# Sparse attention of a float32 two-network kernel: packed fp32r scores, the causal mask as a TensorE product, and one exit for each head

## The chip, the cores and the metric

The kernel runs on one core of one Trainium2 chip, as one launch. The metric is device time in microseconds. The program computes two small transformer networks, one after the other, with two layers each, in float32 on 512 tokens of width 1024.

## What is computed

The part that the change touches is ordinary softmax attention with a causal mask, in three places. The reference of network two's sparse attention, cut to what matters (its compressed branch, the choice of blocks and the window are left out):

```python
q = rope(q.reshape(b, t, N_NSA, D), positions).reshape(b, t, G, R, D)      # 6 heads in 2 groups, D = 64
s_s = einsum('bqgrd,bgqnd->bgrqn', qb, k_sel).astype(f32) * scale          # scores, selected keys
p_s = masked_softmax(s_s, key_pos <= tq[:, None])
o_s = einsum('bgrqn,bgqnd->bqgrd', p_s, v_sel)
s_w = einsum('bqgrd,bngd->bgrqn', qb, kw).astype(f32) * scale              # scores, window keys
p_w = masked_softmax(s_w, m_w)
o_w = einsum('bgrqn,bngd->bqgrd', p_w, vw)
return gt[:, :, 0] * o_c + gt[:, :, 1] * o_s + gt[:, :, 2] * o_w
```

With 512 tokens the kernel treats the selected branch and the window branch both as full causal attention. Network one has a latent attention of 8 heads (causal) and an attention of 4 heads over the best keys of each query (causal, and masked by an index search).

## The kernel before

All tokens lie on 128 partitions in TT = 4 tiles. Big projections run elsewhere, as three fp32r products each (`product`, L262: high by high, high by low, low by high). The attention stages use plain float32.

`softmax_attention` (L2277) is used three times, with the names mla (8 heads, 32 units), dsa (4 heads, 16 units) and nsa (12 heads: 6 for the selected keys and 6 for the window keys; 48 units). A unit is one head and one tile t of 128 queries, with (t + 1) x 128 keys. Each engine has its own instruction list and they meet by semaphores only:

- TensorE, in iteration i: the scores of unit i (L2305) into one of four PSUM banks; the transposes of the probabilities of unit i − 2 (L2314), after ScalarE's exponential of that unit; the product with the values of unit i − 4 (L2325), after ScalarE's copy of the transposed probabilities (L2377), and after the exit of unit i − 6 (`kept`). At the end of a stage come 8 filler transposes (`stay_busy`, L162).
- VectorE, in iteration i: it adds the mask to the last 128 columns of the scores in PSUM (L2340; in dsa to all columns, for tiles above 0), takes the negative maximum (L2341), and then does the exit of unit i − 5: reciprocal of the row sum (L2348), and scaling of the 128x64 result (L2351), or, with a gate, scaling by two factors (L2353) and the addition to what is there (L2354).
- ScalarE, in iteration i: the exponential with its row sum (L2368), then the copy of the transposed probabilities of unit i − 2 (L2377).

After `step(...)` an engine waits for its own instruction.

In network two the stage `turned_and_compressed` (L3087, named cmp) comes before nsa. It turns 15 tiles from token-major to transposed form on TensorE (`turns`: 0 to 3 compressed keys and values, 4 to 6 queries, 7 and 8 selected keys, 9 and 10 window keys, 11 to 14 the queries and keys of the next attention). Even ones are kept by ScalarE (L3221), odd ones by VectorE (L3252). Keys of a group stand twice, once in each half of the partitions, with zeros in the other half that GpSimd clears (L3130), so that a score product runs over 128 rows with two heads' queries in the stationary operand. Then come the compressed attention's scores (L3190, after VectorE's small copy L3263), 26 filler transposes, ScalarE's exponential (L3240), VectorE's mask (L3281), and for each of 6 heads the transposes (L3203), ScalarE's copy (L3243), the product with the values (L3212) and VectorE's exit (L3290, one 128x256 multiplication by a broadcast factor).

## Time and profile before

| | |
|---|---|
| timed runs, median (lowest to highest) of 3 | 3373.87 us (3372.31 to 3375.93) |
| the profiled execution: span | 3368.7 us |
| VectorE busy | 1884.3 us (56% of the span) |
| ScalarE busy | 1311.1 us (39%) |
| nsa, first layer: first score product to last exit | 1666.47 to 1746.16 us |
| nsa, second layer: first score product | 2613.17 us |

The span is that of one execution taken by the hardware profiler; the timed runs are others. The compression stage of the first layer begins at 1624.3 us and that of the second at 2574.1 us. Busy shares of TensorE count a product's whole passage, so a share near 100% does not say that the array works at its peak; the distance from one start to the next says what a product costs in a row of them.

### The profile page before, as it was taken

How to read it: one execution, taken by the hardware profiler on the slowest of the kernel's cores; microseconds unless marked ns; L12 is line 12 of the kernel's file. 1: busy time of each engine (PE TensorE's matmuls, PEld its weight loads, DVE VectorE, ACT ScalarE, POOL GpSimd, SP SyncE). 2: the span in 40 equal slices, each digit the busy share in tenths (PEclk: the TensorE clock that was granted, in tenths of full speed). 3: DMA queues.
4: the chain of work that ended last, by engine and by line, in shares of the span. 5: the costliest groups of instructions: out<-in, count | busy, mean ns of one | idle time of the engine just before them, and what ended most of it. 6: DMA issues, size and time to landing. Idle time of an engine off the chain costs nothing. (4 is left out here: it accounts for less than half of the span.)

```text
span 3368.7 us, 49442 instructions
## 1 busy us (share of the span) xinstructions
PE 3198.9 (95%) x19200; PEld 2657.4 (79%) x19200; DVE 1884.3 (56%) x3610; ACT 1311.1 (39%) x2780; POOL 394.5 (12%) x368
## 2 busy tenths in 40 slices
PE   8998999999989999979999999999899989999996
PEld 6877888877777888868867888888788768888885
DVE  4875443336865434247486457474475865574644
ACT  4455433334354424134363333233443543332324
POOL 1021000000030000003013302010012034010100
PEclk9999999999999999989899999999999999999998
DMA  4111222222102222132100122222222000222221
GB/s 166 54 51 38 88 100 88 88 77 86 66 1 76 100 97 91 38 123 94 51 1 2 40 71 100 97 99 85 81 97 74 1 1 5 91 94 102 91 99 42
DMA packets 37345, 239.58 MB, mean 71 GB/s; under 512 B 4464, under 2 KB 5232, under 8 KB 15088
## 3 DMA queue, kind: packets, MB, share of 16 engines
q1 hardware_dynamic: 36528, 234.21, 19.5%
q8 instruction: 158, 2.59, 0.3%
q10 hardware_dynamic: 576, 2.10, 0.2%
q14 instruction: 83, 0.68, 0.1%
HBM read 234.19 MB, written 2.10 MB: 70 GB/s over the span
## 5 line engine op out<-in xcount | busy, mean ns | idle before, releaser
L265 PE MATMUL ps<-b_hl,bff_whl 128*128 128x512 f32 x704 | 274.1, 389 | 3.1 <-DVE b_hl L630 3.1
L267 PE MATMUL ps<-b_hl,bff_whl 128*128 128x512 f32 x704 | 273.9, 389 | 0.0
L266 PE MATMUL ps<-b_hl,bff_whl 128*128 128x512 f32 x704 | 273.9, 389 | 0.0
L248 DVE SCALAR_TENSOR_TENSOR bff_whl<-ring,b_cols,bff_whl 128x512 fp32r<-128x512 f32 (+1 forms) x224 | 153.2, 745 | 197.3 <-ACT bff_whl L235 197.0
L245 DVE TENSOR_TENSOR aff_whl<-ring,aff_whl 128x512 fp32r<-128x512 f32 x160 | 99.8, 686 | 223.1 <-ACT aff_whl L233 223.1
L235 ACT ACTIVATE bff_whl<-ring,b_cols 128x512 fp32r<-128x512 f32 (+1 forms) x224 | 136.6, 682 | 176.4 <-PE ps L267 176.4
L266 PE MATMUL ps<-aff_whl,a_u 128*128 128x512 f32 x512 | 204.3, 399 | 0.0
L265 PE MATMUL ps<-a_hl,aff_whl 128*128 128x512 f32 x512 | 199.4, 390 | 3.1 <-DVE a_hl L630 3.1
L265 PE MATMUL ps<-aff_whl,a_u 128*128 128x512 f32 x512 | 201.7, 394 | 0.0
L267 PE MATMUL ps<-aff_whl,a_u 128*128 128x512 f32 x512 | 200.7, 392 | 0.0
L266 PE MATMUL ps<-a_hl,aff_whl 128*128 128x512 f32 x512 | 199.2, 389 | 0.0
L267 PE MATMUL ps<-a_hl,aff_whl 128*128 128x512 f32 x512 | 199.2, 389 | 0.0
L265 PE MATMUL ps<-ain_whl,a_hl 128*128 128x512 f32 (+3 forms) x512 | 189.3, 370 | 9.4 <-issue 6.2
L233 ACT CAST aff_whl<-ring 128x512 fp32r<-128x512 f32 x160 | 87.5, 621 | 275.9 <-PE ps L267 271.3
L266 PE MATMUL ps<-ain_whl,a_hl 128*128 128x512 f32 (+3 forms) x512 | 186.2, 364 | 0.0
L267 PE MATMUL ps<-ain_whl,a_hl 128*128 128x512 f32 (+3 forms) x512 | 186.0, 363 | 0.0
L245 DVE TENSOR_TENSOR bff_whl<-ring,bff_whl 128x512 fp32r<-128x512 f32 x128 | 84.6, 720 | 144.2 <-ACT bff_whl L233 144.2
L265 PEld LDWEIGHTS ps<-b_hl,bff_whl 128*128 128x128 f32 x704 | 132.1, 188 | 30.9 <-DVE b_hl L630 3.6
L248 DVE SCALAR_TENSOR_TENSOR aff_whl<-ring,a_gains,aff_whl 128x512 fp32r<-128x512 f32 x128 | 87.6, 746 | 122.3 <-ACT aff_whl L235 122.1
L267 PEld LDWEIGHTS ps<-b_hl,bff_whl 128*128 128x128 f32 x704 | 132.2, 188 | 27.6
L266 PEld LDWEIGHTS ps<-b_hl,bff_whl 128*128 128x128 f32 x704 | 132.2, 188 | 27.3
L233 ACT CAST bff_whl<-ring 128x512 fp32r<-128x512 f32 x128 | 70.4, 621 | 210.3 <-PE ps L267 202.8
(510 smaller groups left out, 7826.8 us busy)
## 6 DMA issues: line engine op xcount, KB each, us to landing
ring<-in_a_w_ff SPq DMA_DIRECT2D x64, 1024.0 KB, 4.6
ring<-in_b_w_up SPq DMA_DIRECT2D x32, 1024.0 KB, 4.8
ring<-in_a_w_in SPq DMA_DIRECT2D x16, 1024.0 KB, 4.9
ring<-in_b_w_down SPq DMA_DIRECT2D x16, 1024.0 KB, 4.6
ring<-in_b_w_in_att SPq DMA_DIRECT2D x12, 1024.0 KB, 4.6
ring<-in_b_w_up SPq DMA_DIRECT2D x16, 768.0 KB, 4.1
ring<-in_b_w_in_conv SPq DMA_DIRECT2D x12, 768.0 KB, 4.2
ring<-in_a_w_out SPq DMA_DIRECT2D x8, 1024.0 KB, 4.7
```

What stands on the lines that cost most here:

```text
L233: self.c.nc.scalar.copy(self.part(j, 0, k), src[:, k, :]).then_inc(self.hi_made, 1)
L235: self.c.nc.scalar.activation(self.part(j, 0, k), src[:, k, :], ACT.Copy, scale=g[:, row + k:row + k + 1]).then_inc(self.hi_made, 1)
L245: self.c.nc.vector.tensor_tensor(self.part(j, 1, k), src[:, k, :], self.part(j, 0, k).bitcast(F32), ALU.subtract).then_inc(self.lo_made, 1)
L248: self.c.nc.vector.scalar_tensor_tensor(out=self.part(j, 1, k), in0=src[:, k, :], scalar=g[:, row + k:row + k + 1], in1=self.part(j, 0, k) ...
L265: nc.tensor.matmul(bank, sh, mh, start=start, stop=False)
L266: nc.tensor.matmul(bank, sh, ml, start=False, stop=False)
L267: return nc.tensor.matmul(bank, sl, mh, start=False, stop=stop)
```

## The change

- `softmax_attention` takes heads instead of units. The results of a head's four tiles go side by side into one PSUM bank (128x256), and VectorE makes one exit for a head, after the maximum of the first tile two heads later: reciprocal of four sums, with a gate a product with it, one multiplication by the broadcast factor and, with a gate, one addition. This holds for mla, dsa and nsa.
- In nsa the queries are split into a high and a low fp32r part, and both stand one above the other in the 128 rows of the stationary operand. The keys' high part stands in both halves, their low part in the half of the queries' high part, with zeros in the other. Two single fp32r products then make a score; the product of the two low parts is not in it.
- In nsa a third fp32r product, the identity by the 128x128 mask, adds the mask in PSUM; VectorE adds none.
- The compression stage makes these operands: ScalarE the high parts, VectorE the low parts, and VectorE copies the identity and the mask to fp32r.

```diff
-def softmax_attention(c, name, units, meanwhile=None, first_act=None):
+class AttentionHead:
+    def __init__(self, scores, values, masks, out, gate=None):
+        self.scores, self.values, self.masks, self.out, self.gate = scores, values, masks, out, gate
+def softmax_attention(c, name, heads, meanwhile=None, first_act=None, mask_product=None):
     nc = c.nc
+    units = [(h, t) for h in range(len(heads)) for t in range(TT)]
     U = len(units)
     with ExitStack() as ctx:
         sb = lambda n, s: ctx.enter_context(nc.sbuf_tensor(name + n, s, F32))
         p, pT = sb("p", [P, 3, SEQ]), sb("pT", [P, 2, SEQ])
-        negmax, rsum, rinv = sb("negmax", [P, 8]), sb("rsum", [P, 8]), sb("rinv", [P, 8])
-        tmp = sb("o", [P, 2, HD])
+        negmax, rsum, weight = sb("negmax", [P, 8]), sb("rsum", [P, 4, TT]), sb("weight", [P, 2, TT])
+        tmp = sb("o", [P, 2, TT, HD])
         with c.stage(name, "scores", "maxed", "probs", "turned", "probsT", "outs", "kept", "step", "pool_step",
                      "act_first") as (
                 block, scores, maxed, probs, turned, probsT, outs, kept, step_sem, pool_step, act_first):
@@ -2299,32 +2311,37 @@
             def _(pe):
                 for i in range(U + 4):
                     if i < U:
-                        qT, kT = units[i][0], units[i][1]
+                        h, t = units[i]
+                        nk = (t + 1) * P
                         if i >= 4:
                             pe.wait_ge(probs, i - 3)
-                        nc.tensor.matmul(c.ps[:, i % 4, 0:kT.shape[1]], qT, kT,
-                                         start=True, stop=True).then_inc(scores, 1)
+                        pairs = heads[h].scores(t)
+                        for n, (q, k) in enumerate(pairs):
+                            ins = nc.tensor.matmul(c.ps[:, i % 4, 0:nk], q, k, start=(n == 0),
+                                                   stop=(n == len(pairs) - 1 and mask_product is None))
+                        if mask_product is not None:
+                            ins = nc.tensor.matmul(c.ps[:, i % 4, nk - P:nk], mask_product[0], mask_product[1],
+                                                   start=False, stop=True)
+                        ins.then_inc(scores, 1)
                     u = i - 2
                     if 0 <= u < U:
-                        nk = units[u][1].shape[1]
                         pe.wait_ge(probs, u + 1)
                         if u >= 2:
                             pe.wait_ge(probsT, u - 1)
-                        for j in range(nk // P):
+                        for j in range(units[u][1] + 1):
                             ins = nc.tensor.transpose(c.ps[:, 4 + u % 2, j * P:(j + 1) * P],
                                                       p[:, u % 3, j * P:(j + 1) * P], c.ident)
                         ins.then_inc(turned, 1)
                     u = i - 4
                     if 0 <= u < U:
-                        nb = units[u][1].shape[1] // P
+                        h, t = units[u]
                         pe.wait_ge(probsT, u + 1)
-                        if u >= 2:
-                            pe.wait_ge(kept, u - 1)
-                        for j in range(nb):
-                            v = units[u][2](j)
-                            ins = nc.tensor.matmul(c.ps[:, 6 + u % 2, 0:v.shape[1]],
-                                                   pT[:, u % 2, j * P:(j + 1) * P], v,
-                                                   start=(j == 0), stop=(j == nb - 1))
+                        if t == 0 and h >= 2:
+                            pe.wait_ge(kept, h - 1)
+                        for j in range(t + 1):
+                            ins = nc.tensor.matmul(c.ps[:, 6 + h % 2, t * HD:(t + 1) * HD],
+                                                   pT[:, u % 2, j * P:(j + 1) * P], heads[h].values(j),
+                                                   start=(j == 0), stop=(j == t))
                         ins.then_inc(outs, 1)
                 c.stay_busy(pe, 0, 8)
@@ -2333,27 +2350,28 @@
                 step = Steps(dve, step_sem)
                 for i in range(U + 5):
                     if i < U:
-                        mask, nk = units[i][3], units[i][1].shape[1]
+                        h, t = units[i]
+                        nk, mask = (t + 1) * P, heads[h].masks(t)
                         dve.wait_ge(scores, i + 1)
-                        nm = mask.shape[1]
-                        s = c.ps[:, i % 4, nk - nm:nk]
-                        step(nc.vector.tensor_tensor(s, s, mask, ALU.add))
+                        if mask is not None:
+                            s = c.ps[:, i % 4, nk - mask.shape[1]:nk]
+                            step(nc.vector.tensor_tensor(s, s, mask, ALU.add))
                         nc.vector.tensor_reduce(negmax[:, i % 8:i % 8 + 1], c.ps[:, i % 4, 0:nk],
                                                 AX.X, ALU.max, negate=True).then_inc(maxed, 1)
                     u = i - 5
-                    if 0 <= u < U:
-                        out, gate, add = units[u][4:7]
-                        ri = rinv[:, u % 8:u % 8 + 1]
+                    if 0 <= u < U and units[u][1] == TT - 1:
+                        h = units[u][0]
+                        head, w = heads[h], weight[:, h % 2, :]
+                        wide = w.unsqueeze(2).broadcast_to([P, TT, HD])
+                        o = c.ps[:, 6 + h % 2, 0:TT * HD].rearrange("p (t d) -> p t d", t=TT)
                         dve.wait_ge(outs, u + 1)
-                        step(nc.vector.reciprocal(ri, rsum[:, u % 8:u % 8 + 1]))
-                        o = c.ps[:, 6 + u % 2, 0:out.shape[1]]
-                        if gate is None:
-                            nc.vector.tensor_scalar(out, o, ri, None, ALU.mult).then_inc(kept, 1)
-                        elif add:
-                            step(nc.vector.tensor_scalar(tmp[:, u % 2, :], o, ri, gate, ALU.mult, ALU.mult))
-                            nc.vector.tensor_tensor(out, out, tmp[:, u % 2, :], ALU.add).then_inc(kept, 1)
+                        step(nc.vector.reciprocal(w, rsum[:, h % 4, :]))
+                        if head.gate is None:
+                            nc.vector.tensor_tensor(head.out, o, wide, ALU.mult).then_inc(kept, 1)
                         else:
-                            nc.vector.tensor_scalar(out, o, ri, gate, ALU.mult, ALU.mult).then_inc(kept, 1)
+                            step(nc.vector.tensor_tensor(w, w, head.gate, ALU.mult))
+                            step(nc.vector.tensor_tensor(tmp[:, h % 2], o, wide, ALU.mult))
+                            nc.vector.tensor_tensor(head.out, head.out, tmp[:, h % 2], ALU.add).then_inc(kept, 1)
             @block.scalar
             def _(act):
@@ -2361,16 +2379,19 @@
                     first_act(act, act_first)
                 for i in range(U + 3):
                     if i < U:
-                        nk = units[i][1].shape[1]
+                        h, t = units[i]
+                        nk = (t + 1) * P
                         act.wait_ge(maxed, i + 1)
                         if i >= 3:
                             act.wait_ge(turned, i - 2)
+                        if t == 0 and h >= 4:
+                            act.wait_ge(kept, h - 3)
                         nc.scalar.activation(p[:, i % 3, 0:nk], c.ps[:, i % 4, 0:nk], ACT.Exp,
                                              bias=negmax[:, i % 8:i % 8 + 1],
-                                             accum_out=rsum[:, i % 8:i % 8 + 1]).then_inc(probs, 1)
+                                             accum_out=rsum[:, h % 4, t:t + 1]).then_inc(probs, 1)
                     u = i - 2
                     if 0 <= u < U:
-                        nk = units[u][1].shape[1]
+                        nk = (units[u][1] + 1) * P
                         act.wait_ge(turned, u + 1)
                         if u >= 2:
                             act.wait_ge(outs, u - 1)
...
+    by_act = [i for i in range(len(turns)) if i % 2 == 0 or i in split]
+    by_dve = [i for i in range(len(turns)) if i % 2 or i in split]
...
-                    for dst, src in halves(i):
-                        ins = nc.scalar.activation(dst, src, ACT.Copy, scale=turns[i][2])
+                    if i in split:
+                        ins = nc.scalar.copy(turns[i][1].hi, c.ps[:, i % 4, :])
+                    else:
+                        for dst, src in halves(i):
+                            ins = nc.scalar.activation(dst, src, ACT.Copy, scale=turns[i][2])
                     ins.then_inc(act_kept, 1)
+                def query_high(f):
+                    r = own_half(f)
+                    nc.scalar.copy(qhl[r, f // 2, f % 2, :], qT[r, f // 2, :]).then_inc(q_his, 1)
...
+                keep(7)
                 keep(8)
                 silu(1)
+                keep(9)
                 keep(10)
                 for i in range(12, len(turns), 2):
                     keep(i)
+                wait_kept(act, 4)
+                wait_kept(act, 5)
+                wait_kept(act, 6)
+                for f in range(2):
+                    query_high(f)
...
+                for f in range(2, H):
+                    query_high(f)
...
+                    if i in split:
+                        dve.wait_ge(act_kept, by_act.index(i) + 1)
+                        keys = turns[i][1]
+                        for b in range(2):
+                            r = own_half(b)
+                            ins = nc.vector.tensor_tensor(keys.lo[r, b, :], c.ps[r, i % 4, :],
+                                                          keys.hi[r, :].bitcast(F32), ALU.subtract)
...
+                def query_low(f):
+                    r, to = own_half(f), other_half(f)
+                    dve.wait_ge(q_his, f + 1)
+                    nc.vector.tensor_tensor(qhl[to, f // 2, f % 2, :], qT[r, f // 2, :],
+                                            qhl[r, f // 2, f % 2, :].bitcast(F32), ALU.subtract).then_inc(q_los, 1)
...
-                for i in (1, 3, 5, 7, 9):
+                for i in (1, 3, 5, 7, 8, 9):
                     keep(i)
                 dve.wait_ge(small, 1)
                 nc.vector.tensor_copy(kcT[:], c.ps[:, SMALL, 128:128 + G * N]).then_inc(small_kept, 1)
+                keep(10)
...
+                for a, b in zip(mask_product, (c.ident, c.causal)):
+                    nc.vector.tensor_copy(a[:], b)
                 for h in range(H):
+                    query_low(h)
                     dve.wait_ge(outs, h + 1)
...
+            qhl = sb1r("qhl", [P, NSA_H // 2, 2, SEQ])
+            khi, klo = sb1r("khi", [P, 2, NSA_G, SEQ]), sb1r("klo", [P, 2, NSA_G, 2, SEQ])
...
+            mask_product = sb1r("identr", [P, P]), sb1r("causalr", [P, P])
...
-                turns += [(twice(a + g * HD), (kT[0:HD, g, 0, :], kT[HD:P, g, 1, :]), 1.0)
-                          for a, kT in ((B_KS, ksT), (B_KW, kwT)) for g in range(NSA_G)]
+                turns += [(twice(a + g * HD), SplitKeys(khi[:, i, g, :], klo[:, i, g]), 1.0)
+                          for i, a in ((0, B_KS), (1, B_KW)) for g in range(NSA_G)]
...
-                pads = [kT[r, :, b, :] for kT in (ksT, kwT) for r, b in ((slice(HD, P), 0), (slice(0, HD), 1))]
-                turned_and_compressed(c, "cmp", turns, pads, cols["w2"], cols["pe"], kv2T, qT, gates, out4)
-            units = []
-            for i, (kT, v) in enumerate(((ksT, B_VS), (kwT, B_VW))):
-                for h in range(NSA_H):
-                    g = h // NSA_R
-                    for t in range(TT):
-                        units.append((qT[:, h // 2, t * P:(t + 1) * P], kT[:, g, h % 2, 0:(t + 1) * P],
-                                      lambda j, v=v, g=g: proj[:, j, v + g * HD:v + (g + 1) * HD], c.causal,
-                                      out4[:, t, h, :], gates[:, t, (i + 1) * NSA_H + h:(i + 1) * NSA_H + h + 1], True))
-            softmax_attention(c, "nsa", units)
+                pads = [klo[r, :, :, b, :].bitcast(F32) for r, b in ((slice(HD, P), 0), (slice(0, HD), 1))]
+                turned_and_compressed(c, "cmp", turns, pads, cols["w2"], cols["pe"], kv2T, qT, qhl, gates, out4,
+                                      mask_product)
+            def packed_scores(i, h):
+                q, g = qhl[:, h // 2, h % 2], h // NSA_R
+                return lambda t: [(q[:, t * P:(t + 1) * P], khi[:, i, g, 0:(t + 1) * P]),
+                                  (q[:, t * P:(t + 1) * P], klo[:, i, g, h % 2, 0:(t + 1) * P])]
+            softmax_attention(c, "nsa", [
+                AttentionHead(packed_scores(i, h),
+                              lambda j, a=v + h // NSA_R * HD: proj[:, j, a:a + HD], lambda t: None,
+                              out4[:, :, h, :], gates[:, :, (i + 1) * NSA_H + h])
+                for i, v in enumerate((B_VS, B_VW)) for h in range(NSA_H)],
+                mask_product=(mask_product[0][:], mask_product[1][:]))
```

## Rows read from the trace of the kernel before

**Rows 1.** Page part 1: busy us of each engine, share of the span, instructions.

```profile
PE 3198.9 (95%) x19200; PEld 2657.4 (79%) x19200; DVE 1884.3 (56%) x3610; ACT 1311.1 (39%) x2780; POOL 394.5 (12%) x368
```

**Rows 2.** Busy by stretch: length, PE, PEld, DVE, ACT, POOL, granted clock, DMA, GB/s.

```profile
1658.00:1667.00 9.00, 8.22 (x36) 6.91 (x36) 1.70 (x4) 1.15 (x2) 0.00 (x0) 0.50 0.00 0
...
1667.00:1677.00 10.00, 9.34 (x41) 6.01 (x39) 6.55 (x21) 5.42 (x19) 0.00 (x0) 0.77 0.01 2
...
1717.00:1727.00 10.00, 9.75 (x60) 7.25 (x60) 8.81 (x34) 6.11 (x20) 0.00 (x0) 1.00 0.00 1
```

**Rows 3.** Timeline, nsa, layer one: start, length, engine, line, instruction, count [idle before].

```profile
1690.44 0.44 PE L2305 MATMUL ps<-b_ksT,b_qT 128*128 128x128 f32 x2
...
1691.24 0.29 DVE L2340 TENSOR_TENSOR ps<-ps,const_b 128x128 f32<-128x128 f32 x1
...
1691.47 0.41 PE L2325 MATMUL ps<-b_proj,nsapT 128*128 128x64 f32 x2 [0.26 <-DVE b_mix L2354]
...
1691.56 0.29 DVE L2341 TENSOR_REDUCE nsanegmax<-ps 128x1 f32<-128x128 f32 x1
...
1691.77 0.15 DVE L2348 RECIPROCAL nsarinv<-nsarsum 128x1 f32<-128x1 f32 x1
...
1692.34 0.23 DVE L2354 TENSOR_TENSOR b_mix<-b_mix,nsao 128x64 f32<-128x64 f32 x1
...
1692.48 0.29 DVE L2340 TENSOR_TENSOR ps<-ps,const_b 128x128 f32<-128x128 f32 x1
...
1696.75 0.44 PE L2305 MATMUL ps<-b_ksT,b_qT 128*128 128x128 f32 x2
```

**Rows 4.** Timeline of mla, first layer.

```profile
221.87 1.08 PE L2305 MATMUL ps<-a_kT,a_qT 96*128 96x512 f32 x2
...
222.78 0.38 PE L2314 MATMUL ps<-const_a,mlap 128*128 128x128 f32 x2
...
223.84 0.44 PE L2305 MATMUL ps<-a_kT,a_qT 96*128 96x128 f32 x2
...
224.12 0.49 PE L2314 MATMUL ps<-const_a,mlap 128*128 128x128 f32 x3
...
227.53 1.08 PE L2305 MATMUL ps<-a_kT,a_qT 96*128 96x512 f32 x2
```

**Rows 5.** Timeline of dsa, second layer.

```profile
1002.70 1.08 PE L2305 MATMUL ps<-a_kbT,a_qbT 128*128 128x512 f32 x2
...
1008.82 1.08 PE L2305 MATMUL ps<-a_kbT,a_qbT 128*128 128x512 f32 x2
```

**Rows 6.** Timeline of the compression stage, second layer: its exit.

```profile
2602.74 0.42 DVE L3290 TENSOR_TENSOR b_mix<-ps,cmpst 128x256 f32<-128x256 f32 x1 [0.80 <-PE ps L3212]
```

**Rows 7.** Timeline of a projection of network two, TensorE alone: products in fp32r.

```profile
1500.11 0.39 PE L267 MATMUL ps<-b_hl,bin_whl 128*128 128x512 f32 x1
...
1500.34 0.39 PE L265 MATMUL ps<-b_hl,bin_whl 128*128 128x512 f32 x1
```

**Rows 8.** Timeline of mla: products with the values.

```profile
223.00 1.00 PE L2325 MATMUL ps<-a_proj,mlapT 128*128 128x64 f32 x8
```

**Rows 9.** Timeline of the compression stage, both layers.

```profile
1656.47 0.62 PE L3203 MATMUL ps<-const_b,cmps 128*31 128x128 f32 x4
...
1658.14 1.06 PE L3203 MATMUL ps<-const_b,cmps 128*31 128x128 f32 x4
...
1661.02 1.06 PE L3203 MATMUL ps<-const_b,cmps 128*31 128x128 f32 x4
...
2589.76 1.39 DVE L3252 TENSOR_SCALAR b_kwT<-ps 64x512 f32<-64x512 f32 x2 [4.34 <-PE ps L3147]
...
2590.63 1.20 ACT L3221 ACTIVATE b_kwT<-ps 64x512 f32<-64x512 f32 x2 [1.40 <-PE ps L3147]
...
2598.40 0.82 ACT L3240 ACTIVATE cmps<-cmps 128x744 f32<-128x744 f32 x1
...
2600.90 1.05 ACT L3243 COPY cmppT<-ps 31x512 f32<-31x512 f32 x2 [1.68 <-PE ps L3203]
```

More of the change, by code:

```diff
@@ L3084, in _, with __init__, turned_and_compressed @@
                     dve.wait_ge(states, t + 1)
-def turned_and_compressed(c, name, turns, pads, w2, pe_tiles, kv2T, qT, gates, out):
+class SplitKeys:
+    def __init__(self, hi, lo):
+        self.hi, self.lo = hi, lo
+def turned_and_compressed(c, name, turns, pads, w2, pe_tiles, kv2T, qT, qhl, gates, out, mask_product):
     nc = c.nc
+    split = [i for i in range(len(turns)) if isinstance(turns[i][1], SplitKeys)]
+    by_act = [i for i in range(len(turns)) if i % 2 == 0 or i in split]
+    by_dve = [i for i in range(len(turns)) if i % 2 or i in split]
     H, G, N = NSA_H, NSA_G, N_CMP
@@ L3108, in turned_and_compressed, with own_half, other_half @@
         with c.stage(name, "turned", "act_kept", "dve_kept", "pe_here", "biased", "silus", "small", "small_kept",
[L3109 removed]
+                     "scores", "step", "centred", "exps", "masked", "p_turned", "p_kept", "outs", "outs_kept", "padded", "q_his", "q_los") as (
                 block, turned, act_kept, dve_kept, pe_here, biased, silus, small, small_kept, scores, step_sem, centred,
[L3111 removed]
+                exps, masked, p_turned, p_kept, outs, outs_kept, padded, q_his, q_los):
             def wait_kept(engine, i):
[L3113 to L3116 removed]
+                if i in by_dve:
+                    engine.wait_ge(dve_kept, by_dve.index(i) + 1)
+                else:
+                    engine.wait_ge(act_kept, by_act.index(i) + 1)
+            def own_half(f):
+                return slice(HD * (f % 2), HD * (f % 2 + 1))
+            def other_half(f):
+                return slice(HD * (1 - f % 2), HD * (2 - f % 2))
             def halves(i):
@@ L3555, in first_block @@
                 softmax_attention(c, "mla", [
-                    (qT[0:MLA_QK, h, t * P:(t + 1) * P], kT[0:MLA_QK, h, 0:(t + 1) * P],
-                     lambda j, h=h: kv4[:, j, h, MLA_NOPE:], c.causal,
-                     mix[:, t, h * MLA_V:(h + 1) * MLA_V], None, False)
-                    for h in range(MLA_H) for t in range(TT)], other_ropes)
+                    AttentionHead(lambda t, h=h: [(qT[0:MLA_QK, h, t * P:(t + 1) * P],
+                                                   kT[0:MLA_QK, h, 0:(t + 1) * P])],
+                                  lambda j, h=h: kv4[:, j, h, MLA_NOPE:], lambda t: c.causal,
+                                  mix[:, :, h * MLA_V:(h + 1) * MLA_V])
+                    for h in range(MLA_H)], other_ropes)
             with ExitStack() as ctx3:
@@ L3584, in first_block @@
                           lambda dve, step, i: search.late(dve, step, i, TOPK // 8 - SEARCH_EARLY))
-                units = []
-                for h in range(DSA_H):
-                    for t in range(TT):
-                        mask = c.causal if t == 0 else search.tile(t)
-                        units.append((qbT[:, h // 2, t * P:(t + 1) * P],
-                                      kbT[:, h % 2, 0:(t + 1) * P],
-                                      lambda j: proj[:, j, A_AV:A_AV + DSA_D], mask,
-                                      mix[:, t, o_b + h * DSA_D:o_b + (h + 1) * DSA_D], None, False))
+                sparse = [AttentionHead(lambda t, h=h: [(qbT[:, h // 2, t * P:(t + 1) * P],
+                                                         kbT[:, h % 2, 0:(t + 1) * P])],
+                                        lambda j: proj[:, j, A_AV:A_AV + DSA_D],
+                                        lambda t: search.tile(t) if t else c.causal,
+                                        mix[:, :, o_b + h * DSA_D:o_b + (h + 1) * DSA_D]) for h in range(DSA_H)]
                 junk = sb3("junk", [P, HD])
@@ L3601, in last_spread @@
                                              accum_out=var[:, t, h:h + 1]).then_inc(spreads, 1)
-                softmax_attention(c, "dsa", units,
+                softmax_attention(c, "dsa", sparse,
                                   lambda pool, step: group_norm(nc, pool, step, out4, heads(A_RG, RET_H, RET_D),
@@ L3713, in attentions @@
                           for a, dst, s in ((B_SQ, sqT, HD ** -0.5), (B_SK, skT, 1.0)) for i in range(SB_H // 2)]
-                pads = [kT[r, :, b, :] for kT in (ksT, kwT) for r, b in ((slice(HD, P), 0), (slice(0, HD), 1))]
-                turned_and_compressed(c, "cmp", turns, pads, cols["w2"], cols["pe"], kv2T, qT, gates, out4)
-            units = []
-            for i, (kT, v) in enumerate(((ksT, B_VS), (kwT, B_VW))):
-                for h in range(NSA_H):
-                    g = h // NSA_R
-                    for t in range(TT):
-                        units.append((qT[:, h // 2, t * P:(t + 1) * P], kT[:, g, h % 2, 0:(t + 1) * P],
-                                      lambda j, v=v, g=g: proj[:, j, v + g * HD:v + (g + 1) * HD], c.causal,
-                                      out4[:, t, h, :], gates[:, t, (i + 1) * NSA_H + h:(i + 1) * NSA_H + h + 1], True))
```

13 lines of the change are left out of this document (5 added, 8 removed).

## The prediction, made before the kernel was changed

> **What bounds the kernel now.** I read the page's busy line first: the reader is to see TensorE at 95% of the span and VectorE at 56% [rows 1]. The chain of waits was no help, since it stays within the last microsecond of the program. An average over two networks does not say what one attention stage is worth, so I read busy time by stretches. In network two's sparse attention (the stage named nsa, twice in the span, 48 units of work each time) TensorE is 9.75 of 10 us busy and VectorE 8.81 of 10; the stretch just before it stands at a granted clock of 0.50, that is 1.2 GHz [rows 2].
>
> Two engines near full need the timeline. One head (four units, one for each tile of 128 queries) takes 1696.75 − 1690.44 = 6.31 us of nsa. In it the probabilities-by-values product waits for VectorE's last write [0.26 <-DVE b_mix] [rows 3]. VectorE's starts there give what one exit (reciprocal, scaling, addition) costs: reciprocal to addition 0.57, addition to the next mask addition 0.14, sum 0.71 us; and mask addition to maximum 0.32 us. The same loop in network one's first attention (mla), with a shorter exit and nothing waiting, runs a head in 227.53 − 221.87 = 5.66 us [rows 4]. There one step follows another on TensorE: the score product of 128 keys takes 0.28 us and that of 512 keys 0.91 us; between them on a line, 0.49 and 0.70 for 256 and 384, together 2.38 us. The rest, 5.66 − 2.38 = 3.28 us, is transposes and products with the values. So mla is TensorE's own pace, and nsa is 0.65 us a head over that pace because of VectorE. The top-k attention (dsa) takes 1008.82 − 1002.70 = 6.12 us a head, 0.46 over it, with the same VectorE in front: its mask additions are wide [rows 5].
>
> **The change, part by part.**
>
> *Mask and exits leave VectorE.* In nsa, four mask additions go (4 × 0.32 = 1.28 us a head) and four exits become one. The new exit is a reciprocal (0.15 as in [rows 3], 0.19 with the wait for its own end), a product with the gate on four numbers a row (about the same, 0.19), a 128x256 multiplication out of PSUM by a broadcast factor, which the compression stage already does in 0.42 us [rows 6], and an addition of the same size, 0.42 at most: 1.22 us with no waits, against 4 × 0.71 = 2.84. VectorE had 6.31 × 0.881 = 5.6 us a head; it now has 5.6 − 1.28 − 1.62 = 2.7 us. It cannot be the bound any more.
>
> *Scores.* Each full float32 product goes as two TensorE instructions. The new score is two single-pass fp32r products over all 128 rows, and a third of 128 columns for the mask. The big products of the kernel run in fp32r at 1500.34 − 1500.11 = 0.23 us for 512 columns, 0.44 ns a column [rows 7]. The six wide products of a head (2 × (256 + 384 + 512) = 2304 columns) cost 1.02 us. The six narrow ones (two scores of 128 keys, four masks) have no row in fp32r. Bounds: 0.057 us each by columns alone; 0.28 us if a narrow fp32r product is worth a whole float32 one [rows 4]. The nearest row is the value product: eight loads of 128x128 weights with 64 columns each take 1.00 us [rows 8]; two of them take 0.41 [rows 3], so a pair of load and product is (1.00 − 0.41)/6 = 0.10 us, set by the load. I take 0.107: 0.64 us for six. Scores are then 1.66 us, with 0.1 for seams 1.76. A head of TensorE: 3.28 + 1.76 = 5.04 us.
>
> The Trainium skill (TensorE: Matmul & The Clock Gate, section on the back-to-back issue gap) has pairs of load and product of 128 columns at about 81 ns. By that the six cost 0.49 us, and the whole change would bring some 3 us more; my row is of float32 weights and doesn't settle it.
>
> *Does anything else take TensorE's place?* ScalarE is the candidate: four exponentials with their sums and four copies. I laid one head out in TensorE's order (scores of unit i, transposes of i − 2, values of i − 4). The delicate point is the exit, now 1.22 us in one piece between the maxima of tiles 0 and 1. The second maximum ends 2.4 us after the head's start, the exponential 0.5 later, and the transposes that need it come at 4.0. The copy of tile 3 ends at 3.5 and is needed at 4.2. Slack is 0.6 us or more everywhere, so I take 5.04 us. Gain 6.31 − 5.04 = 1.27 a head. Eleven heads run in the steady state (the first fills the pipe at the low clock): 14.0 us, and 1.0 for shorter scores in the filling. The last exit, uncovered at the end of the stage, is 1.22 against 0.71: −0.5. Per layer 14.5 us, for two layers **29.0 us gained**.
>
> *mla and dsa* get only shared exits. In mla TensorE was never kept waiting: nothing. Its last exit is longer by 0.14 us and lies beside the filler transposes. In dsa VectorE falls below TensorE's 5.66, so 0.46 × 3 heads after filling × 2 layers = **2.8 us gained**.
>
> *The compression stage pays for the operands.* Keys are kept by both ScalarE (high part, one copy of 128x512 instead of two of 64x512) and VectorE (low part, two subtractions of 64x512). ScalarE's two copies took 1.20 us, so one is 0.6; VectorE's pair 1.39 [rows 9]. The last key tile's low part now starts after its high part: the small copy of compressed keys behind it, which TensorE's compressed scores await, is late by 0.6 us. Then two query copies stand in ScalarE's queue ahead of the exponential: 1.2 us. Four more (2.4 us) stand between the exponential and the first probability copy. These started 2600.90 − 2598.40 = 2.50 after one another; now the exponential's 0.82 plus 2.4 make 3.22: 0.7 more. Sum 2.5 us. VectorE's query remainders (0.69 each, one a head) and the two copies of the mask's operands (0.3 each, as the 128x128 mask addition) fit in its waits for TensorE of 0.8 to 2.5 us: nothing, and if that cover were gone 0.7 us a head. GpSimd clears the same bytes with half the instructions.
>
> The price has a second part. TensorE waits some 2 us longer in that stage with its fillers used up, and the granted clock there already falls to half [rows 2]. One head's step there took 1.67 us just before (1656.47 to 1658.14) and 2.88 after (to 1661.02) [rows 9]; each step that falls under the low clock earlier costs 1.2 us. I take one a layer, bounds 0 and 3. The skill's page just named, in the section on the clock gate, says that throttled is the default and activity releases it; taken alone, that speaks against this change, since it makes TensorE idle. It would give the upper bound, 3.7 us a layer; the trace shows also that the clock had fallen in a stretch with TensorE 8.22 of 9 us busy, so idling alone is not all of it. Together 2.5 + 1.1 = 3.6 us a layer, **7.2 us lost** (5 to 12.5).
>
> **Sum.** −29.0 − 2.8 + 7.2 = −24.6 us on the profiled 3368.7: 3344.1 us of span. The median of the timed runs, 3373.87, is 5.2 over that span; I carry it over: 3349 us.
>
> **Rivals.**
> - *Narrow fp32r runs at four cycles a column* (0.23 us, what 512 columns cost now). For it: float32 takes that much per column. Against: nothing in the trace has fp32r under 256 columns. Heads at 5.04 + 6 × 0.12 = 5.76; 15.8 us less gain over 22 heads: 3365 us.
> - *The exit in one piece stalls the pipe.* If my slack is wrong by more than 0.6 us, the loop is paced by maximum, exit, maximum, exponential, copy, and loses about 0.5 us a head: 3360 us. For it: TensorE waited for VectorE before. Against: the layout above.
> - *It does not do what it says*: the narrow products cost a whole float32 product, 0.28 us. Scores are 1.02 + 1.68 + 0.1 = 2.80, more than the 2.38 removed; a head takes 6.08, gain 0.23, and the compression stage eats it: 3372 us, no change.
> - *Slower:* nsa's TensorE stays at 1.2 GHz. The stage starts at half clock and the mean rose to 0.77 in its first 10 us [rows 2], under dense float32 passes. Lighter fp32r work in its place with gaps might not raise it. TensorE's 5.04 then becomes about 10 us: 5 lost on each head that stays low. It decides from about five heads of 24 (24.6/5) on; all of a layer would be 3400 us. Against: the fp32r layers run at full clock throughout.
>
> **How the numbers follow.** Forecast 0.66, its own range 3341 to 3356. Four cycles a column 0.13; stalling exit 0.10; whole float32 price 0.07; low clock 0.04. Between 3340 and 3366 lies all of the first three but their edges. A change of 0.2% (6.7 us) is about what a measurement can tell here: faster 0.87, same 0.08, slower 0.05.
>
> **What would show it.** In the profile after: no mask addition of nsa on VectorE and 24 exits of 128x256; a head of nsa at 5.0 us, with no wait of the value products on VectorE; 128-column fp32r starts 0.11 apart; mla's head still 5.66, dsa's near 5.7; the compression stage 2.5 to 6 us longer, with ScalarE's query copies ahead of its exponential. A head above 5.5 us, or a nsa stretch with granted clock under 1.0 beyond its first 10 us, makes the prediction wrong.

## The result, and the profile after

The changed kernel takes 3342.74 us (median of 4 runs, 3337.18 to 3348.88), the kernel before on the same chip 3374.43 (4 runs, 3372.31 to 3375.93): ratio 0.9915 [0.9897, 0.9933], 31.7 us less. Timed twice more, each time beside the kernel before, it took 3357.00 (12 runs, 3346.07 to 3364.95; before 3365.66, ratio 0.9963 [0.9947, 0.9979]) and 3353.58 (6 runs, 3344.83 to 3359.12; before 3369.39, ratio 0.9949 [0.9929, 0.9969]). So the gain is 9, 16 or 32 us, and the forecast of 25 lies between. The scatter is not measuring noise alone: TensorE's granted clock falls for some microseconds at places that the change does not touch, in some executions and not in others.

The page of the kernel after, part 1 (compare [rows 1]):

```profile
span 3335.4 us, 49102 instructions
...
PE 3166.2 (95%) x19296; PEld 2662.0 (80%) x19296; DVE 1816.9 (54%) x3202; ACT 1313.6 (39%) x2792; POOL 393.7 (12%) x364
```

VectorE lost 408 instructions and 67 us of work; TensorE stays at 95%. Stretches of nsa, first layer, columns as in [rows 2]:

```profile
1662.00:1671.00 9.00, 8.22 (x36) 7.03 (x36) 3.76 (x7) 1.15 (x2) 0.00 (x0) 0.50 0.00 0
1671.00:1681.00 10.00, 10.00 (x68) 9.72 (x68) 4.67 (x12) 6.97 (x25) 0.00 (x0) 0.77 0.01 2
...
1701.00:1711.00 10.00, 10.00 (x89) 9.84 (x88) 6.18 (x18) 7.20 (x24) 0.00 (x0) 1.00 0.01 2
```

TensorE is busy 10.00 of 10 us, where it was 9.75; VectorE 6.18, where it was 8.81. The entry at half clock and the rise in the first 10 us are as before. One head of nsa in the timeline (columns as in [rows 3]):

```profile
1694.28 0.31 PE L2320 MATMUL ps<-b_khi,b_qhl 128*128 128x128 f32 x1
...
1694.42 0.27 PE L2320 MATMUL ps<-b_klo,b_qhl 128*128 128x128 f32 x1
...
1694.54 0.28 PE L2323 MATMUL ps<-b_causalr,b_identr 128*128 128x128 f32 x1
...
1694.65 0.52 PE L2332 MATMUL ps<-const_b,nsap 128*128 128x128 f32 x3
...
1695.46 0.42 DVE L2373 TENSOR_TENSOR nsao<-ps,nsaweight 128x256 f32<-128x256 f32 x1
...
1695.92 0.42 DVE L2374 TENSOR_TENSOR b_mix<-b_mix,nsao 128x256 f32<-128x256 f32 x1
...
1697.54 0.47 PE L2320 MATMUL ps<-b_khi,b_qhl 128*128 128x512 f32 x1
...
1697.85 0.39 PE L2320 MATMUL ps<-b_klo,b_qhl 128*128 128x512 f32 x1
1697.85 0.19 PEld L2323 LDWEIGHTS ps<-b_causalr,b_identr 128*128 128x128 f32 x1
1698.07 0.22 PE L2323 MATMUL ps<-b_causalr,b_identr 128*128 128x128 f32 x1
...
1698.13 0.39 PE L2332 MATMUL ps<-const_b,nsap 128*128 128x128 f32 x2
...
1699.17 0.31 PE L2320 MATMUL ps<-b_khi,b_qhl 128*128 128x128 f32 x1
```

A head is 1699.17 − 1694.28 = 4.89 us, no mask addition is left on VectorE, and no TensorE row waits. Where the time went, by stages, in us for each layer. The marks are starts of instructions: compression runs from its first one to nsa's first maximum, nsa from there to the first row of the stick-breaking attention behind it ("stick") that writes its scores to SBUF, and stick from there to its last addition in PSUM; "rest" is all else:

| kernel | compression | nsa | stick | rest | span |
|---|---|---|---|---|---|
| before | 43.3 + 40.2 | 79.6 + 79.2 | 45.9 + 45.0 | 3035.5 | 3368.7 |
| after | 46.9 + 46.0 | 63.5 + 63.4 | 40.3 + 41.9 | 3033.4 | 3335.4 |

nsa gave 31.9 us and the compression stage took 9.4: together 22.5. A further 8.7 came from stick, whose code is the same; no part of the forecast had it.

### The profile page after: what moved, and what is told of

Read it like the earlier page. It is cut to its first block and busy times, and to the rows that moved or that the text cites. A ratio compares the mean times of both kernels' runs of the same rounds, so it can differ in the third digit from the quotient of the medians.

```text
span 3335.4 us, 49102 instructions
## 1 busy us (share of the span) xinstructions
PE 3166.2 (95%) x19296; PEld 2662.0 (80%) x19296; DVE 1816.9 (54%) x3202; ACT 1313.6 (39%) x2792; POOL 393.7 (12%) x364
```

## The experiments

### Which of the three edits does it (six kernels)

**Shared exits alone**, on the kernel before; scores and mask additions stay:

```diff
-                    if 0 <= u < U:
+                    if 0 <= u < U and units[u][1] == TT - 1:
...
-                        step(nc.vector.reciprocal(ri, rsum[:, u % 8:u % 8 + 1]))
+                        step(nc.vector.reciprocal(w, rsum[:, h % 4, :]))
```

> The kernel before with the shared exits alone, in all three attention stages; scores in plain float32, mask on VectorE. Theory (nsa was held by VectorE's waits, and TensorE's own pace with float32 scores is 5.66 us a head): VectorE falls from 5.6 to about 4.0 us a head, a head of nsa takes 5.66 instead of 6.31, 22 heads in the steady state give 14 us less: about 3360 us. dsa unchanged, as in the changed kernel. Rival (the exit in one piece stalls the loop as single exits did): nsa's head stays above 6.1 us, no change, 3374 us.

**Mask product alone**, on the kernel before:

```diff
+                        if mask_product is not None:
+                            ins = nc.tensor.matmul(c.ps[:, i % 4, nk - P:nk], mask_product[0], mask_product[1],
+                                                   start=False, stop=True)
...
-                        step(nc.vector.tensor_tensor(s, s, mask, ALU.add))
+                        if mask_product is None:
+                            step(nc.vector.tensor_tensor(s, s, mask, ALU.add))
```

> The kernel before with the mask product alone in nsa: a float32 score, then the fp32r identity product; exits one for each unit. Theory: VectorE loses 1.28 us a head and TensorE gains 4 narrow products at 0.06 to 0.11 us, so its pace is 5.9 to 6.1 against 6.31 before: 5 to 9 us less, about 3367 us. Rival (the time came from VectorE alone, a narrow product costs nothing beside it): the head takes 5.66, 14 us less, 3360 us. Rival (the mask product belongs on VectorE, TensorE being the bound): no gain at all.

**The changed kernel with the mask back on VectorE**:

```diff
-                              lambda j, a=v + h // NSA_R * HD: proj[:, j, a:a + HD], lambda t: None,
+                              lambda j, a=v + h // NSA_R * HD: proj[:, j, a:a + HD], lambda t: c.causal,
...
-                mask_product=(mask_product[0][:], mask_product[1][:]))
```

> The changed kernel with the mask back on VectorE in nsa (packed scores and shared exits stay; the mask's operands are still copied). Theory (TensorE paces nsa at 4.89 us a head): four narrow products fewer, TensorE's pace is 4.5 to 4.65, VectorE has 2.7 + 1.3 = 4.0 us and stays below it: nsa some 5 us shorter a stage pair than the changed kernel's, 3337 us. Rival (the mask addition ahead of the maximum lengthens the chain from scores to exponential, which then paces the loop): head 4.9 us or more, 3343 us or above.

**The changed kernel with one exit a unit**:

```diff
-                            ins = nc.tensor.matmul(c.ps[:, 6 + h % 2, t * HD:(t + 1) * HD],
+                            ins = nc.tensor.matmul(c.ps[:, 6 + u % 2, 0:HD],
...
-                    if 0 <= u < U and units[u][1] == TT - 1:
...
+                    if 0 <= u < U:
```

> The changed kernel with one exit for each unit again, in all three attention stages (packed scores and the mask product stay in nsa). Theory: VectorE has 2.84 + 1.6 = 4.4 us a head in nsa, under TensorE's 4.89, but the value products wait again for single exits; a head takes 4.9 to 5.2, 0 to 7 us more, 3343 to 3350 us; dsa's head is as before the change (6.12). Rival (shared exits bring the main part of the gain): the head takes over 5.5 us, 13 us more or worse, 3356 us.

Measured on one chip (before 3368.82): 3353.89, ratio 0.9952 [0.9934, 0.9970]; 3358.57, 0.9968 [0.9948, 0.9988]; 3353.17, 0.9955 [0.9934, 0.9976]; 3351.31, 0.9954 [0.9934, 0.9974]. The times hardly separate the four; the steady step from one head to the next in the traces does. Two more kernels fill the table (**shared exits and mask product on float32 scores**, and **packed scores alone**; edits as above, combined; 3366.78 and 3380.27 us, one run each):

> The kernel before with shared exits and the mask product in nsa, scores in plain float32: VectorE is relieved twice, TensorE paces. Theory (a mask product costs TensorE 0.045 us): a head takes 5.65 + 0.18 = 5.83 us, slower than the 5.65 of shared exits alone. Rival (0.107 us each, as the prediction had it): 6.08 us. Rival (the mask off VectorE still helps): under 5.65 us.

> The changed kernel with packed scores alone: one exit for each unit and the mask on VectorE, as before the change. Theory (VectorE's 5.6 us a head is then the bound): a head takes 5.6 to 5.8 us, since VectorE no longer waits for scores. Rival (the waits of the value products for single exits stay): 6.3 us as before.

| us a head | one exit a unit | shared exit |
|---|---|---|
| float32 scores, mask on VectorE | 6.30 (before) | 5.65 |
| float32 scores, mask product | 5.83 | 5.77 |
| packed scores, mask on VectorE | 5.92 | 5.23 |
| packed scores, mask product | 5.15 | 4.89 (after) |

Against their expectations: shared exits alone (5.65) and one exit a unit (5.15) came out by their theories; the mask product alone (5.83) and both on float32 scores (5.77) came out 0.06 to 0.07 below theirs; packed scores alone (5.92) lie above the theory's 5.6 to 5.8 and under its rival's 6.3; with the mask back on VectorE the theory (4.5 to 4.65) failed and the rival holds (5.23).

With float32 scores the shared exit alone brings nsa to mla's pace (5.66, [rows 4]), TensorE's own; there the mask product only adds work, 5.77 − 5.65 = 0.12 us for four, 0.03 each. Packed scores alone bring 6.30 − 5.92 = 0.38 us a head, where they bring 5.77 − 4.89 = 0.88 beside the other two edits, for VectorE stays in front; the timeline of that kernel's TensorE shows the wait of [rows 3] again:

```profile
1692.97 0.85 PE L2342 MATMUL ps<-b_proj,nsapT 128*128 128x64 f32 x6 [0.23 <-DVE b_mix L2375]
```

With the mask back on VectorE, TensorE has four products less and the head is 0.34 us longer. In its timeline the wait is for ScalarE:

```profile
1696.26 0.28 PE L2320 MATMUL ps<-b_klo,b_qhl 128*128 128x256 f32 x1
...
1697.16 0.42 DVE L2374 TENSOR_TENSOR b_mix<-b_mix,nsao 128x256 f32<-128x256 f32 x1
...
1697.51 0.29 DVE L2358 TENSOR_TENSOR ps<-ps,const_b 128x128 f32<-128x128 f32 x1
...
1697.83 0.42 DVE L2359 TENSOR_REDUCE nsanegmax<-ps 128x1 f32<-128x256 f32 x1
...
1698.29 0.47 ACT L2389 ACTIVATE nsap<-ps,nsanegmax 128x256 f32<-128x256 f32 x1 [1.04 <-DVE nsanegmax L2359]
...
1698.76 0.57 ACT L2398 COPY nsapT<-ps 128x512 f32<-128x512 f32 x1
...
1699.48 0.41 PE L2332 MATMUL ps<-const_b,nsap 128*128 128x128 f32 x2 [0.46 <-ACT nsapT L2398]
```

VectorE is busy 4.08 of 5.23 us here (window 1690.00 to 1695.23), so on average it has time for the mask. But the scores of the second tile are done at 1696.54 and their mask addition starts at 1697.51, behind the exit in one piece. From there ScalarE's exponential, which waited 1.04 us for the maximum, and ScalarE's copy behind it lead to TensorE's wait. So here the exit in one piece does stand in the path, and the mask addition behind it lengthens it. In the changed kernel the second tile's maximum starts at 1696.26, right behind the exit's last row (1695.92 0.42), and TensorE does not wait. How much of the 0.34 us is the exit's place and how much the addition itself was not isolated.

By stages, both layers: shared exits alone take 12.3 us off nsa (146.4 against 158.7) and add nothing to the compression stage (82.4 against 83.5). Packed scores alone take 10.3 off nsa (148.4) and put 13.6 on the compression stage (97.1 against 83.5): alone they do not pay. All three give 22.5. No timing sets the whole change above shared exits alone, which took 14.9 us less than the kernel before on their chip, against 31.7, 8.7 and 15.8 for the whole; only the stages do (22.5 against 12.3 in nsa).

### Is the first timing's extra gain the change's? (the same kernel again)

> The changed kernel itself, timed on one chip with the next ones and profiled once more. The profile first taken gained 8.7 us in the stick-breaking stage, which the change doesn't touch: its granted clock stood at 1.00 where it had fallen to 0.50 before. Theory (the fall is a matter of phase): this profile may show it in either layer, stick stages of 40 to 46 us, and the median is some 24 us under that of the kernel before (the stages nsa and cmp alone: −31.9 + 9.4). Rival (the change steadies that clock): both stick stages at 40 to 42 us again, and some 31 us less. nsa 63.5 us in both layers by either.

> The changed kernel once more, timed beside the next one. By its stages (nsa −32, cmp +10 to +12, the rest clock) it should stand 20 us under the kernel before in the median; the two timings so far gave 32 and 9. Theory (both are one effect under the scatter of the granted clock): 12 to 28 us less. Rival (the small one is right, the first was luck): under 12 us less.

The first stands 8.7 us under the kernel before, short of its theory's 24; the second 15.8, inside its theory's 12 to 28. Their heads are 4.89 and their nsa stages 63.9, 63.4, 63.5 and 63.4 us, as in the first profile. But the spans are 3350.3 and 3355.4, since other stages are longer: of the 15.0 us between the first two profiles 5.4 lie before the first compression stage (1624.3 and 1629.7) and 5.6 in the first stick stage (40.3 and 45.9). That stage in windows of 4 us; first before, then after, then the changed kernel again, first layer, and last the third timing's second layer (10 us):

```profile
1759.00:1763.00 4.00, 2.98 (x9) 1.95 (x8) 3.53 (x9) 2.88 (x6) 1.41 (x4) 0.66 0.00 0
1763.00:1767.00 4.00, 4.00 (x14) 3.21 (x15) 1.95 (x5) 2.21 (x6) 3.83 (x3) 0.50 0.00 0
```

```profile
1747.00:1751.00 4.00, 2.36 (x11) 1.75 (x11) 3.35 (x9) 3.29 (x7) 1.83 (x4) 1.00 0.00 0
1751.00:1755.00 4.00, 4.00 (x27) 3.10 (x26) 2.25 (x5) 2.22 (x7) 3.83 (x3) 1.00 0.00 0
```

```profile
1753.00:1757.00 4.00, 2.98 (x9) 1.77 (x8) 3.53 (x6) 2.39 (x6) 0.71 (x2) 0.80 0.00 0
1757.00:1761.00 4.00, 4.00 (x12) 2.86 (x11) 2.66 (x7) 2.81 (x8) 3.40 (x4) 0.50 0.00 0
```

```profile
2695.00:2705.00 10.00, 10.00 (x17) 4.42 (x17) 5.26 (x14) 5.51 (x12) 2.07 (x4) 0.50 0.00 1
```

The same code runs at 1.2 or at 2.4 GHz (0.50, 1.00), and the very same kernel does both. So the 8.7 us in stick are not shown to be the change's.

### The compression stage's bill, and the clock

**The query copies moved** behind the exponential and between the probability copies, and the small copy of compressed keys ahead of the last key tile's low part:

```diff
-                for f in range(2):
-                    query_high(f)
...
+                    if 1 <= h < H - 1:
+                        query_high(h + 1)
...
-                for i in (1, 3, 5, 7, 8, 9):
+                for i in (1, 3, 5, 7, 8):
...
+                keep(9)
```

> The changed kernel, with no query copy ahead of ScalarE's exponential in the compression stage: two behind it, the other four between the probability copies; on VectorE the last key tile's low part behind the small copy that the compressed scores wait for. Theory (ScalarE's queue is what lengthened the stage, 2.5 us a layer by the prediction's sum): the stage returns from 46.9 and 46.0 us to 41 to 43, 8 to 10 us less in all. Rival (the granted clock sets the stage's length, the copies are hidden): 45 us or more, under 3 us less.

**The same, with fillers** in the last five heads' steps of that stage:

```diff
+                    if h >= 2:
+                        c.stay_busy(pe, 3, 4)
```

> The kernel of the run just before, with 20 more filler transposes of 128x128 in the compression stage, four ahead of each of the last five heads' steps. Theory (TensorE loses its clock there because it waits and works on 31 rows): the clock stays at 1.00 to the stage's end and into nsa, a step stays at 1.6 to 1.7 us instead of 2.9, and the stage is 3 to 5 us shorter a layer, nsa 1 to 2 us. Rival (the fillers are only more work): the clock falls as before, and the stage is 2 to 4 us longer.

**The changed kernel, with fillers in stick**, 16 transposes in two of its waits for VectorE:

```diff
+                    if i in (5, 7):
+                        c.stay_busy(pe, 7, 8)
```

> The changed kernel with 16 filler transposes in the stick-breaking stage, in two of its waits for VectorE 10 to 14 us after its start. Theory (the fall of the clock there comes from those waits): no fall in either layer, both stages at 40 us, and the run-to-run spread of the whole smaller. Rival (the fall is not from waits): stages of 42 us or more as in other profiles.

Beside 3357.00 for the changed kernel and 3365.66 for the one before on that chip they took 3344.55 (0.9928 [0.9908, 0.9948]), 3350.44 (0.9946 [0.9922, 0.9971]) and 3343.16 (0.9918 [0.9898, 0.9939]). TensorE's timeline in the first compression stage; before, after, and with the copies moved:

```profile
1638.81 1.97 PE L3147 MATMUL ps<-const_b,b_proj 128*64 128x128 f32 x32
...
1653.86 1.10 PE L3212 MATMUL ps<-cmpvcmp,cmppT 31*128 31x64 f32 x8 [0.23 <-ACT cmppT L3243]
```

```profile
1638.80 1.97 PE L3186 MATMUL ps<-const_b,b_proj 128*64 128x128 f32 x32
...
1642.42 4.09 PE L3229 MATMUL ps<-cmpkcT,b_qT 64*128 64x31 f32 x48 [0.61 <-DVE cmpkcT L3332]
...
1656.25 1.10 PE L3251 MATMUL ps<-cmpvcmp,cmppT 31*128 31x64 f32 x8 [1.00 <-ACT cmppT L3298]
```

```profile
1638.01 1.97 PE L3186 MATMUL ps<-const_b,b_proj 128*64 128x128 f32 x32
...
1653.06 1.10 PE L3251 MATMUL ps<-cmpvcmp,cmppT 31*128 31x64 f32 x8 [0.23 <-ACT cmppT L3296]
```

From the start of the last key products to the first value product it is 15.05 us before, 17.45 after and 15.05 moved: the 2.40 us are the two queues' order, and both new waits are gone. In the second layer the same distance is 12.91, 16.11 and 13.87. The stages are then 42.8 + 44.5 us instead of 46.9 + 46.0, 5.6 us less in all: under the theory's 8 to 10, over the rival's 3. Of the 4.3 us that the second layer keeps over the 40.2 of before, 0.96 lie in that distance. There ScalarE loads the table for its exponential behind the wait for VectorE; before the change the load stood beside it (first before, then moved):

```profile
2597.02 0.93 DVE L3276 TENSOR_TENSOR cmps<-cmps,cmpst 128x744 f32<-128x744 f32 x1
...
2597.11 1.28 ACT L3240 ACT_TABLE_LOAD   x1
```

```profile
2572.66 0.93 DVE L3347 TENSOR_TENSOR cmps<-cmps,cmpst 128x744 f32<-128x744 f32 x1
...
2573.69 1.28 ACT L3291 ACT_TABLE_LOAD   x1 [0.97 <-DVE cmps L3347]
```

The other 3.3 come with the second layer's clock, here with the copies moved (columns as in [rows 2]):

```profile
2579.00:2585.00 6.00, 6.00 (x27) 4.75 (x27) 2.83 (x5) 2.57 (x5) 0.00 (x0) 0.51 0.00 0
2585.00:2591.00 6.00, 6.00 (x27) 4.97 (x27) 2.38 (x5) 1.76 (x3) 0.00 (x0) 0.50 0.00 0
```

The fillers there gave 42.2 + 49.2. In the first layer the clock still stands at 1.00 from 1664 to 1668, 36 to 40 us into the stage, where it was 0.50 without them. In the second it falls where it fell without them, 29 us into the stage, and the stage is 4.7 us longer: the rival's fall, at more than its price of 2 to 4. The fillers in stick gave 40.3 + 40.3, and no row under 1.00. Their kernel's median is 13.8 us under the changed one's; stick accounts for 7.3 of them in the two profiles (80.6 us against 87.8), the rest is open.

**Both together**, moved copies and fillers in stick:

> The changed kernel with both changes that helped: the query copies out of the way of ScalarE's exponential, and 16 fillers in the stick-breaking stage. Theory (they work in different stages and add): 3.5 us a layer in cmp and no fall of the clock in the stick-breaking stage, 15 to 20 us under the changed kernel, about 3335 us. Rival (the gains of each were the same scatter): no more than 10 us under the changed kernel.

It took 3332.91 us (6 runs, 3330.12 to 3341.93), beside 3353.58 for the changed kernel, 20.7 us less, and 3369.39 for the one before: ratio 0.9902 [0.9882, 0.9921]. Its stages: compression 41.6 + 42.6, nsa 63.4 + 63.4, stick 40.3 + 40.3. It beats both kernels.

## Why the prediction was right

**VectorE was nsa's bound, and leaves.** Right: no value product waits for it. The 2.7 us a head came out at 0.618 × 4.89 = 3.0, still far off.

**The head, 5.04 us.** Measured 4.89. The scores are 0.37, 0.39, 0.50 and 0.59 us for the four tiles, 1.85, against 1.76 taken. Two errors in that term partly cancel. The six narrow products are cheap, 0.56 us against 0.64: 0.11 to 0.14 at 128 keys and 0.06 to 0.07 for a mask behind a wide one, its weights loading beneath that one (load and product start at 1697.85 and 1698.07). The wide ones are dear, 1.29 against 1.02, and their first product above all: 0.31 for 512 columns in place of 0.23 [rows 7], 0.22 for the second. The rest, 10 transposes and 20 value products, is 4.89 − 1.85 = 3.04, where 3.28 was carried over from mla: 0.101 us a pair of load and product. The mis-sized term is that one; 0.15 × 22 = 3.3 us more gain, near the 31.9 measured against 29.0. Why such a pair costs less here than in mla (3.28/30 = 0.109) no run shows. The Trainium skill (TensorE: Matmul & The Clock Gate, back-to-back issue gap) has about 81 ns for a pair with 128 columns; by it 30 pairs would be an estimated 2.4 us, and the 3.04 of this trace do not agree.

**The shared exit does not stall, slack 0.6 us.** Right in nsa.

**dsa falls to TensorE's pace, 2.8 us.** Wrong. The forecast took VectorE's load as all that held dsa. Its timeline after:

```profile
1002.78 1.08 PE L2320 MATMUL ps<-a_kbT,a_qbT 128*128 128x512 f32 x2
...
1003.90 0.70 DVE L2358 TENSOR_TENSOR ps<-ps,a_score 128x512 f32<-128x512 f32 x1 [0.48 <-PE ps L2320]
...
1004.63 0.69 DVE L2359 TENSOR_REDUCE dsanegmax<-ps 128x1 f32<-128x512 f32 x1
...
1005.36 0.69 ACT L2389 ACTIVATE dsap<-ps,dsanegmax 128x512 f32<-128x512 f32 x1 [1.08 <-DVE dsanegmax L2359]
...
1005.78 0.17 DVE L2368 RECIPROCAL dsaweight<-dsarsum 128x4 f32<-128x4 f32 x1
...
1006.04 0.36 ACT L2398 COPY dsapT<-ps 128x256 f32<-128x256 f32 x1
...
1006.54 0.63 PE L2332 MATMUL ps<-const_a,dsap 128*128 128x128 f32 x4 [0.36 <-ACT dsapT L2398]
...
1008.83 1.08 PE L2320 MATMUL ps<-a_kbT,a_qbT 128*128 128x512 f32 x2
```

6.05 us a head, not 5.7, though VectorE is busy 4.30 of them. A wait for the copy of the probabilities has taken the place of the wait for VectorE. The rows above are its chain: the 512 wide mask addition, the maximum, the exponential, the copy of 256 behind it on ScalarE. The exit starts at 1005.78, when that maximum is done, and so is not in this chain; no run takes the wide addition out. From one head's first maximum to the next it is 7.00, 6.05 and 6.04 us in the second layer, against 5.70, 6.43 and 6.12 before. The last two steps are 0.46 shorter together, but the last head gives most of it back. The first step is the clock's: 7.00 in the first layer of before too, with 0.54 granted in 992.50 to 999.50 after and 1.00 from 996.00 on before. From the first to the last maximum it is 24.2 + 24.2 us against 24.3 + 23.0, and 22.9 where the second layer's first step is 5.70 (shared exits alone): 0.1 a layer, where 1.4 was forecast. mla's, 41.9 + 41.9 against 42.0 + 42.0, are as forecast.

**The compression stage, 7.2 us.** Measured 9.4, inside the bounds of 5 to 12.5. Over seven profiles with the packed operands, the copies where the change has them, it is 92.9 to 98.0 us for both layers, over four without 82.3 to 83.5 (mean 82.9): 10 to 12 us more in five, 14 and 15 in two, beyond the upper bound. The queue part was 2.40 and 3.20 against 2.5. In the second layer its three terms are 0.69 for the small copy (0.6 forecast), 1.73 at the exponential (1.2) and 0.78 between exponential and first copy (0.7); the middle one is the mis-sized one, for the table load of 1.28 us stands behind the two query copies and no longer beside VectorE's work. The clock part was 3.6 − 2.4 = 1.2 in the first layer, as forecast (1.1), and 5.8 − 3.2 = 2.6 in the second, and over the profiles it varies most.

**The rivals.** The stalling exit falls for nsa as changed, where no TensorE row waits; with the mask on VectorE the exit is in the path. Four cycles a column, and the whole float32 price, fall with the 0.06 to 0.14 us of the narrow products. A low clock in nsa falls: 1.00 from the second 10 us on.

**The sum.** nsa and compression gave 22.5 us against 21.8 forecast, since 2.9 too little in nsa and 2.2 too little in the compression stage cancel; the total of 24.6 also held the 2.8 of dsa. That closeness is partly luck. The first timing's larger gain holds the clock of untouched stages, and so does the second's smaller one; the first is inside the likeliest case's own range, the second 1 us above it, all in the full range. A forecast of such a kernel to less than some 10 us would need the clock's falls, which nothing in the trace of before foretells.

## What to carry to other kernels

- When two engines are near full, price each edit with the others made: beside shared exits the mask product costs 0.12 us a head when scores are long, and brings 0.34 when they are short. Beside single exits it brings 0.47 and 0.77.
- An engine with time to spare on average can still be late in one stretch: look at what stands in its queue ahead of the instruction that others await, and follow that chain in every stage that shares the code.
- An operand prepared ahead of a loop is paid in the queue in which it is prepared; put such copies behind the instruction that another engine awaits.
- Judge a change of half a per cent by its stages in several profiles, not by one timing.

## What the hardware showed that was not expected

For the same kernel the granted clock falls in one execution and not in another. In stick it fell in a stretch with waits (TensorE 2.98 of 4 us busy, mean clock 0.66) and stood at 0.50 through the next, which is full (4.00 of 4); in the kernel after, a stretch with 2.36 of 4 us busy kept 1.00. A full row at 0.50 holds less work: 14 products where 27 fill the same 4 us at 1.00. In the third timing TensorE is busy 10.00 of 10 us at 0.50, so a full row alone does not bring the clock back. Sixteen filler transposes in two waits held it at 1.00 in four of four stick stages in two profiled kernels. Of the other twelve profiles nine have a stage of 44.9 us or more there, and six of their 24 stages took 40.3 us without such fillers. The Trainium skill (TensorE: Matmul & The Clock Gate, section "What's actually happening") ties the clock to how busy TensorE has been; the fillers agree. Why one execution falls and another does not stays open, and so does whether the packed operands make the falls in the compression stage likelier.

ScalarE's table load takes 1.28 us and can lie beside another engine's work or in the path: in the second compression stage its place was worth 0.96 us.
